# Two-layer transformer on one core: the q of layer 2's attention, and half of its k, are turned by VectorE and by transfers of lane quarters

## What is computed

```python
proj = h @ w_in[l]                          # 256 x 8704
qa, ka, va, qb, kb, vb, ga, gb = split(proj)
qa = apply_rope(rms_norm(qa, q_norm_w), cos, sin)   # 8 heads of 128
ka = apply_rope(rms_norm(ka, k_norm_w), cos, sin)   # 2 heads
ya = global_gqa(qa, ka, va)                 # 4 q heads share a k and a v head
yb = neighbourhood_attention(qb, kb, vb, rpb)       # 8 heads, a bias per head
merged = sigmoid(ga) * (ya @ w_oa) + sigmoid(gb) * (yb @ w_ob)
x = x + g1 * (merged @ w_out)               # then the feed-forward part
```

## Time and profile before

| | |
|---|---|
| Runs | 2236.20, 2235.26, 2235.86 us; median 2235.86 |
| Profiled execution | 2235.32 us, span 2233.6 us |
| TensorE busy | 2220.6 us (99%) |
| VectorE busy | 1680.4 us (75%) |
| ScalarE busy | 1104.4 us (49%) |
| Moved by DMA | 546.53 MB, mean 245 GB/s |

### The profile page before, as it was taken

The page is one execution under the profiler, slowest core; times in us unless marked ns, Lnnn a source line. Parts: engine busy times, 40 slices in busy tenths (PEclk is TensorE's granted clock), DMA queues, the critical chain, the costliest instruction groups (busy, mean ns, idle before and its releaser), DMA issues.

```text
span 2233.6 us, 31176 instructions
## 1 busy us (share of the span) xinstructions
PE 2220.6 (99%) x10287; PEld 1848.6 (83%) x10287; DVE 1680.4 (75%) x2250; ACT 1104.4 (49%) x1427; POOL 136.9 (6%) x259
## 2 busy tenths in 40 slices
PE   9999999999999999999999999999999999999998
PEld 7888888888888888888888888888888888888886
DVE  5767777878876875887788877767777777777786
ACT  6455445666664444533366653445444443444444
POOL 1100110000000000010011110000000000000000
PEclk9999999999999999999999999999999999999999
DMA  8978897666665866697689987766666676766664
GB/s 303 340 240 301 312 337 244 209 208 204 216 230 185 286 233 200 213 335 269 197 299 320 323 293 252 243 210 217 220 213 223 229 234 227 231 218 213 202 210 147
DMA packets 150219, 546.53 MB, mean 245 GB/s; under 512 B 16881, under 2 KB 17648, under 8 KB 148608
## 3 DMA queue, kind: packets, MB, share of 16 engines
q1 hardware_dynamic: 112416, 405.92, 53.7%
q0 software_dynamic: 34304, 129.64, 16.9%
q10 hardware_dynamic: 3424, 9.96, 1.1%
HBM read 534.92 MB, written 10.53 MB: 244 GB/s over the span
## 4 chain that ended last, share of the span: by engine, by line
PE 98%; DVE 1%; DMA 0%; ACT 0%; issue 0%; DVEq 0%; ACTq 0%; SPq 0%
PE ps L2072 23%; PE ps L2074 23%; PE ps L2073 23%; PE ps L2190 7%; PE ps L2192 7%; PE ps L2191 7%; PE ps L2111 2%; PE ps L2320 1%; PE ps L2087 1%; PE ps L2089 1%; PE ps L2088 1%; PE ps L2387 0%; PE ps L2388 0%; PE ps L2250 0%; PE ps L2315 0%; PE ps L2510 0%
## 5 line engine op out<-in xcount | busy, mean ns | idle before, releaser
L668 ACT ACTIVATE w_hi<-raw 128x1024 fp32r<-128x1024 f32 x749 | 790.1, 1060 | 967.7 <-PE ps L2074 820.4
L1175 DVE TENSOR_TENSOR w_lo<-raw,w_hi 128x1024 fp32r<-128x1024 f32 x757 | 922.0, 1223 | 450.5 <-ACT w_hi L668 437.3
L2072 PE MATMUL ps<-w_hi,a_hi 128*128 128x512 f32 x1612 | 629.3, 390 | 0.0
L2074 PE MATMUL ps<-w_hi,a_lo 128*128 128x512 f32 x1612 | 627.5, 389 | 0.0
L2073 PE MATMUL ps<-w_lo,a_hi 128*128 128x512 f32 x1612 | 627.3, 389 | 0.0
L2074 PEld LDWEIGHTS ps<-w_hi,a_lo 128*128 128x128 f32 x1612 | 302.5, 188 | 63.4
L2072 PEld LDWEIGHTS ps<-w_hi,a_hi 128*128 128x128 f32 x1612 | 302.6, 188 | 62.9 <-DVE a_lo L1460 0.3
L2073 PEld LDWEIGHTS ps<-w_lo,a_hi 128*128 128x128 f32 x1612 | 302.6, 188 | 61.9
L2190 PE MATMUL ps<-w_hi,a_hi 128*128 128x512 f32 x640 | 255.4, 399 | 0.0
L2192 PE MATMUL ps<-w_hi,a_lo 128*128 128x512 f32 x640 | 249.7, 390 | 0.0
L2191 PE MATMUL ps<-w_lo,a_hi 128*128 128x512 f32 x640 | 249.2, 389 | 0.0
(11 more groups left out here) (366 smaller groups left out, 2318.6 us busy)
## 6 DMA issues: line engine op xcount, KB each, us to landing
raw<-ws_dram SPq DMA_DIRECT2D x768, 512.0 KB, 4.4
ada<-wa_dram POOLq DMA_DIRECT2D x140, 512.0 KB, 4.9
late<-wa_dram POOLq DMA_DIRECT2D x35, 512.0 KB, 5.5
late_c<-wa_dram POOLq DMA_DIRECT2D x17, 512.0 KB, 5.4
gates_spill<-gst ACTq DMA_DIRECT2D x16, 512.0 KB, 5.4
ga<-gates_spill POOLq DMA_DIRECT2D x8, 512.0 KB, 4.3
gb<-gates_spill POOLq DMA_DIRECT2D x8, 512.0 KB, 5.6
bias_c<-b_merge_dram POOLq DMA_DIRECT2D x9, 256.0 KB, 5.8
```

The source lines that it names most:

```text
L668: act.activation(w_hi[:, k.slot(RING), :], raw[:, k.slot(RING), :], ACT.Copy).then_inc(hi_done, 1)
L1175: dve.tensor_tensor(w_lo[:, k.slot(RING), :], raw[:, k.slot(RING), :], w_hi[:, k.slot(RING), :].bitcast(F32), ALU.subtract).then_inc(lo_do ...
L2072: pe.matmul(o, hi(m, tb), w_hi[:, s, cols], start=m == 0, stop=False)
L2074: mm = pe.matmul(o, lo(m, tb), w_hi[:, s, cols], start=False, stop=m == of * kts - 1)
```

## The change

Five steps are changed.

1. When a chunk of q or of neighbourhood k lies in `proj`, VectorE transposes it in blocks of 32 x 32, each inside its own quarter of the lanes, into a buffer `qz` of two slots: one instruction of 128 x 512 for each half of the tokens (`q_lanes_turned`). The chunks come in the order 3, 4, 5, 0, 1, 6 (`LANES2`).
2. ScalarE waits for that (`q_lanes`) and issues 16 DMAs of 32 lanes x 1 KB, from a quarter of `qz` into a quarter of `proj[:, c]` (`quadrants`, `steps_sending`), four ahead of each of four splits. Blocks and quarters together make the 128 x 128 turn. The transfers are sent in chunks 4 to 8, one in each of chunks 4 to 7 and two in chunk 8.
3. TensorE no longer turns q in any of the four groups, nor k in the neighbourhood groups. The k of the grouped-query groups stays with it.
4. ScalarE rounds q and k from `proj` (SBUF) with a strided view, by halves of the tokens; VectorE takes the low parts from there too. Their count is the same. TensorE waits for `qk2_split` ahead of the scores.
5. Loops of ScalarE and VectorE in `proj2` are written out, and one wait of gpsimd, ScalarE's waits ahead of q_hi and of `pt_hi` (which lies on `qz`) are put to the new semaphores.

```diff
+        qz = at("qz", SC + 8 * K, [P, 2, 4, TB, 4, 32])
+        def heads_first(c):
+            return proj[:, c].rearrange("p t n -> p (t n)").rearrange("p (i t h s) -> p t h i s", i=4, t=TB, h=4)
+        def lanes(x, tb):
+            return x[:, :, tb * P:(tb + 1) * P].rearrange("p h (i s) -> p h i s", i=4)
...
-        gqa = Attention("gqa", 2, 1, 2 + 4)
-        na = Attention("na", 2, 1, 2 + 2 + 4)
+        gqa = Attention("gqa", 2, 1, 4)
+        na = Attention("na", 2, 1, 4)
+        SPLIT2 = {"gqa": (0, 2), "na": (2 * gqa.groups, 4)}
+        LANES2 = (3, 4, 5, 0, 1, 6)
+        TURN_DMAS = 4 * 4 * 16
...
                     if m == 3 * N_LATE + 1:
-                        pool.wait_ge(t_done, TG["na"] + 4)
+                        pool.wait_ge(qk2_split, SPLIT2["na"][0] + 4)
...
# ScalarE, attention
+                else:
+                    if a.kind == "gqa" and g.base == 0:
+                        act.wait_ge(q_turned[0], 2 * TURN_DMAS)
+                        act.wait_ge(q_turned[1], 3 * TURN_DMAS)
+                    elif g.base == 0:
+                        act.wait_ge(gqa.qk_done, len(gqa.units) * gqa.groups)
+                    else:
+                        act.wait_ge(a.qk_done, nu)
+                    for tb in range(TB):
+                        act.activation(lanes(q_hi, tb), heads_first((3 if na_ else 0) + i)[:, tb], ACT.Copy).then_inc(qk2_hi, 1)
...
                 if na_:
-                    for h in range(2):
-                        act.wait_ge(t_done, (r + 1).n)
-                        act.activation(k2_hi[:, 2 * h:2 * h + 2, :], ps[:, 4 + r.slot(2), :], ACT.Copy)\
-                            .then_inc(qk2_hi, 1)
-                        r = r + 1
+                    act.wait_ge(q_turned[0], 3 * TURN_DMAS)
+                    for tb in range(TB):
+                        act.activation(lanes(k2_hi, tb), heads_first(5 + i)[:, tb], ACT.Copy).then_inc(qk2_hi, 1)
...
                     elif j and not nsa_:
+                        act.wait_ge(q_turned[0], 3 * TURN_DMAS)
...
# ScalarE, projection
-            with act.Fori(1, 6) as i:
+            def quadrants(n):
+                act.wait_ge(q_lanes, n + 1)
+                s = (n + 1) % 2
+                turned = proj[:, LANES2[n]].rearrange("p t n -> p (t n)").rearrange("p (i r) -> p i r", i=4)
+                z = qz[:, s].rearrange("p b t h s -> p b (t h s)")
+                def column(b):
+                    for i in range(4):
+                        act.dma_start(turned[32 * b:32 * b + 32, i, :], z[32 * i:32 * i + 32, b, :]).then_inc(q_turned[s], 16)
+                return column
+            def steps_sending(k, n):
+                column = quadrants(n)
+                for b in range(4):
+                    column(b)
+                    steps(k + b, 1)
+            with act.Fori(1, 4) as i:
                 steps(At(T0["proj2"], T_K, i), T_K)
+            k = At(T0["proj2"] + 4 * T_K)
+            steps(k, 3)
+            steps_sending(k + 3, 0)
+            steps(k + 7, 1)
+            k = k + T_K
+            steps(k, 1)
+            steps_sending(k + 1, 1)
+            steps(k + 5, 3)
...
+            k = k + T_K
+            steps_sending(k, 4)
+            steps_sending(k + 4, 5)
...
# VectorE, projection
+            def q_lanes_turned(n):
+                c, s = LANES2[n], (n + 1) % 2
+                if n >= 2:
+                    dve.wait_ge(q_turned[s], n // 2 * TURN_DMAS)
+                for tb in range(TB):
+                    ins = dve.transpose(qz[:, s, :, tb], proj[:, c, tb].rearrange("p (h b f) -> p b h f", h=4, b=4))
+                ins.then_inc(q_lanes, 1)
...
             for c in range(3):
                 k, g = k + T_K, g + 1
+                dve.wait_ge(acc_free, G0["proj2"] + 5 + c + 3)
+                q_lanes_turned(2 + c)
                 steps(At(k), 2)
                 qk_scaled(c)
                 steps(At(k + 2), 2)
                 qk_turned(c, 0)
+                if c == 2:
+                    q_lanes_turned(5)
                 steps(At(k + 4), 2)
                 qk_turned(c, 1)
                 steps(At(k + 6), 2)
...
# TensorE, attention
-                for h in range(2):
-                    turn(r, [q[:, tb, 2 * h + m, :] for m in range(2) for tb in range(TB)]).then_inc(t_done, 1)
-                    r = r + 1
+                if nsa_:
+                    for h in range(2):
+                        turn(r, [qr[:, tb, 2 * h + m, :] for m in range(2) for tb in range(TB)]).then_inc(t_done, 1)
+                        r = r + 1
...
-                if na_:
-                    k_ = proj[:, 5 + i].rearrange("p t (h d) -> p t h d", h=4)
-                    for h in range(2):
-                        turn(r, [k_[:, tb, 2 * h + m, :] for m in range(2) for tb in range(TB)]).then_inc(t_done, 1)
-                        r = r + 1
...
                 else:
+                    pe.wait_ge(qk2_split, SPLIT2[a.kind][0] + SPLIT2[a.kind][1] * (g.base + 1))
                     pe.wait_ge(proj_in, 1)
```

More of the change, by code:

```diff
@@ L349, in build @@
         qk2_hi, v2_hi_done, v2_split, pt_hi_done = sem("qk2_hi"), sem("v2_hi_done"), sem("v2_split"), sem("pt_hi_done")
+        q_lanes, q_turned, qk2_split = sem("q_lanes"), [sem(f"q_turned{k}") for k in range(2)], sem("qk2_split")
         hdn_ready, hdnT_done, hdnT_ready, w2_in = sem("hdn_ready"), sem("hdnT_done"), sem("hdnT_ready"), sem("w2_in")
@@ L1318, in k_rest @@
                 def k_rest():
-                    for h in range(2):
-                        hs = slice(2 * h, 2 * h + 2)
-                        rest(k2_lo[a.kind][:, hs, :], 2 + h, 4 + (TG[a.kind] + g.base * a.tg + h) % 2, k2_hi[:, hs, :], t_free)
+                    for tb in range(TB):
+                        rest(lanes(k2_lo[a.kind], tb), 2 + tb, heads_first(5 + i)[:, tb], lanes(k2_hi, tb), qk2_split)
                 def p_rest(j):
@@ L1326, in p_rest @@
                         dve.wait_ge(pt_hi_done, u + 1)
-                        dve.tensor_tensor(pt_lo[:, n, :], ps[:, 4 + (TG["gqa"] + g.base * a.tg + 2 + 2 * (j - 1) + n) % 2, :],
+                        dve.tensor_tensor(pt_lo[:, n, :], ps[:, 4 + (TG["gqa"] + g.base * a.tg + 2 * (j - 1) + n) % 2, :],
                                           pt_hi[:, n, :].bitcast(F32), ALU.subtract).then_inc(t_free, 1)
@@ L1783, in _ @@
             n = ADA_TURN["proj2"][0]
-            with dve.Fori(0, 2) as i:
-                for c in range(2):
-                    k = At(T0["proj2"] + (c + 1) * T_K, 2 * T_K, i)
-                    steps(k, T_K, At(ADA0["proj2"] + c * n // 2, n, i), n // 2, c * n // 2)
-                    copy_out(2 * i + (c + 1), k, At(G0["proj2"] + (c + 1), 2, i))
-                keep_modulation(At(ADA0["proj2"], n, i), n, At(KEPT0["proj2"], 1, i))
+            def q_lanes_turned(n):
+                c, s = LANES2[n], (n + 1) % 2
+                if n >= 2:
+                    dve.wait_ge(q_turned[s], n // 2 * TURN_DMAS)
+                for tb in range(TB):
+                    ins = dve.transpose(qz[:, s, :, tb], proj[:, c, tb].rearrange("p (h b f) -> p b h f", h=4, b=4))
+                ins.then_inc(q_lanes, 1)
+            for i in range(2):
+                for c in range(2):
+                    k = At(T0["proj2"] + (2 * i + c + 1) * T_K)
+                    a, na_ = At(ADA0["proj2"] + i * n + c * n // 2), n // 2
+                    if (i, c) == (1, 1):
+                        steps(k, 2, a, 2, c * n // 2)
+                        dve.wait_ge(acc_free, G0["proj2"] + 3 + 3)
+                        q_lanes_turned(0)
+                        steps(k + 2, T_K - 2, a + 2, na_ - 2, c * n // 2 + 2)
+                    else:
+                        steps(k, T_K, a, na_, c * n // 2)
+                    copy_out(2 * i + (c + 1), k, At(G0["proj2"] + (2 * i + c + 1)))
+                keep_modulation(At(ADA0["proj2"] + i * n), n, At(KEPT0["proj2"] + i))
             dve.wait_ge(trig2_in, 32)
@@ L2200, in attention @@
                 fill(a.fill[0] - between)
-                q = qr if nsa_ else proj[:, (3 if na_ else 0) + i].rearrange("p t (h d) -> p t h d", h=4)
                 if not na_:
                     pe.wait_ge(a.q_ready, (g + 1).n)
-                for h in range(2):
-                    turn(r, [q[:, tb, 2 * h + m, :] for m in range(2) for tb in range(TB)]).then_inc(t_done, 1)
-                    r = r + 1
+                if nsa_:
+                    for h in range(2):
+                        turn(r, [qr[:, tb, 2 * h + m, :] for m in range(2) for tb in range(TB)]).then_inc(t_done, 1)
+                        r = r + 1
                 if not na_:
```

31 lines of the change are left out of this document (17 added, 14 removed).

## The result

The changed kernel takes 2240.86 us in the median of eleven executions (2238.1 to 2243.9) against 2235.86 for the kernel before, a ratio of 1.0020 with a 95% interval of 1.0012 to 1.0029. It is slower by 0.2%, where the prediction said 2230.8 us (range 2229.9 to 2234.8) and had 0.50 on faster. The profiled execution took 2238.95 us, its span 2237.1.

A forecast was written before the change was run, and what follows sets the result against it. TensorE, busy for 99% of the span, was taken to bound the kernel. From the median 2235.86 us, 5.5 saved, 0.3 added for the k-turn wait and 0.1 for the scores gave 2230.8 us, range 2229.9 to 2234.8.

The forecast's parts named there:

- What is added: Part pricing the new work: VectorE's twelve transposes at 0.70 us, ScalarE's 96 DMA issues at 0.36 us, and resulting waits.
- the bound of 0.50: ScalarE's DMA issue: upper bound of 0.50 us each, from the 256-row issue and a gap.
- the far bound of 0.68: ScalarE's DMA issue: extreme of 0.68 us each, from the gpsimd row and a gap.
- the lane quarters: VectorE's transposes: quarters one after another, about 2.3 us each, losing about 13.5 us; 0.10 together with slow issues.
- the walk through chunk 8: New order laid on old starts, tile by tile: first gate tile's split 0.9 us ahead of need, k turns wait 0.3.
- slower by the issues: Rival: issues at 0.68 us lose 12 us in chunks 5 to 8 and first group, 2242.8; 0.10 with slow quarters.
- The saving: TensorE without 48 of the 52 turns reading `proj`: 5.5 us saved (5.3 to 5.7), all on the path.
- the two kept turns: Two turns of grouped-query k staying on TensorE in each of its two groups, taken at 0.30 us.
- the low parts: VectorE's low parts of q and k in the attention: as many as before, at 0.68 us.
- the landing: Last gqa q transfer issued by 1102.7, wanted at 1117.4; rival that transfers land late, 2253 us, had 0.04.
- the increment that runs ahead of the copy: `gqa_q_ready` before the k turns: VectorE's sequencer runs ahead, so it comes at 1115.7 to 1116.6, TensorE waiting 0 to 0.6.
- I cost it at nothing, and 0.5 us at worst: Weight loads in the shorter neighbourhood groups: DMA engines always wanted, but tiles still over 2 us ahead of TensorE.

The follow-up runs named there:

- e_order: Changed kernel with one rounding put ahead of each wait for the transposed lanes in chunk 8, all issues still on ScalarE: 2235.72 us, ratio 0.9995.
- e_fill: Changed kernel plus 16 extra matmuls on TensorE, result unused, ahead of the first gate tile: 2242.93 us, ratio 1.0029.
- e_last: Changed kernel with only chunk 8's two transfers (32 issues) moved from ScalarE to GpSimd: 2231.91 us, ratio 0.9978.
- e_pool: Changed kernel with all 96 transfers issued by GpSimd instead of ScalarE: 2231.96 us, ratio 0.9978.
- e_order_fill: `e_order` plus eleven extra matmuls, result unused, behind the first gate tile where TensorE stood for 2.5 us: 2234.67 us, ratio 0.9999.
- e_second: `e_last` with the second transfer of chunk 8 (16 issues) back on ScalarE: 2236.61 us, ratio 1.0005.

## Why the prediction was wrong

**The step that failed** is in "What is added": "with a gap between two I take 0.36 us, so 1.44 us for four". It is 0.612 us and 2.44 to 2.46 us. I had scaled a single issue to DRAM by the number of its rows, and the rows don't count. The true value lies between the bound of 0.50 and the far bound of 0.68, to which I gave a tenth with the lane quarters. Everything in the walk through chunk 8 follows from that term: with 0.612 us in it the same walk has the second transfer at 1112.2 and the split of the first gate tile at 1115.7 (an estimate), near the measured 1112.52 and 1116.15. ScalarE still keeps pace in steady state (2.56 us from rounding to rounding against 2.72), since it does issue while it works. But the first wait puts it 2.44 us behind instead of 1.4, and the second transfer starts at 1112.52 instead of 1108.8. The split of the first gate tile starts at 1116.15, where 1111.4 was forecast and 1113.46 is when its result is needed. `gqa.q_ready` comes at 1123.9 instead of 1115.7 to 1116.6. The rival "slower by the issues" had the mechanism and, at 0.68 us, 2242.8 (its 12 us lost add up to 2242.4).

**The term that was missing** is the granted clock behind a gap. It made the second loss in chunk 8's timeline, which the wait for the k turn covers in the first profile of the changed kernel (nothing in the sum). In the second profile it adds 1.3 us, in `e_order` 1.2, in `e_fill` 2.5.

**One distance orders the versions without the turns.** It is the one from the time at which the first gate matmul is due (the last projection matmul and 0.227 us, or its start where it is on time) to the first score matmul, in the profiled execution. The third column is the median of `e_last` and the difference of the distances.

| version | distance, us | 2231.91 and the difference | median measured |
|---|---|---|---|
| `e_last` | 8.44 | | 2231.91 |
| `e_pool` | 8.43 | 2231.9 | 2231.96 |
| `e_order_fill` | 11.57 | 2235.0 | 2234.67 |
| `e_order` | 12.76 | 2236.2 | 2235.72 |
| `e_second` | 13.48 | 2236.9 | 2236.61 |
| changed kernel, two executions | 16.55, 17.87 | 2240.0, 2241.3 | 2240.86 |
| `e_fill` | 19.27 | 2242.7 | 2242.93 |

The medians come out within 1 us. But the distance is that of one execution, the medians are of several sets, and single executions differ by more in other places: from its own profiled times (2230.97 for `e_last`) the same sum gives 2236.0 for `e_second`, measured 2233.65, and 2234.1 for `e_order_fill`, measured 2231.97. So the table shows that the loss is in this stretch, and not its size to some tenths.

Of the changed kernel's 16.55 - 8.44 = 8.1 us, 4.05 are the first gap, 2.4 the slow tile, 1.3 the wait for the k turn and 0.3 what follows. With `e_fill` and `e_pool` together it is shown that the first three are one delay, ScalarE's, under which a shorter gap only makes a longer wait.

**What held.** The saving: in the changed kernel itself the second grouped-query group takes 8.44 us from gate to scores (1172.83 to 1181.27), and the neighbourhood groups 10.88 and 10.98 (1224.07 to 1234.95, 1275.95 to 1286.93), where the earlier trace rows has 9.30, 12.70 and 12.90. The first group in `e_pool` takes 8.43. That is 0.87 + 0.86 + 1.82 + 1.92 = 5.5 us, the forecast value, and the two kept turns are 8.44 - 8.16 = 0.28 (forecast 0.30). The transposes at 0.692 us (0.70), the low parts at 0.685, the landing (ScalarE rounds q at 1124.66 right behind its last weight rounding, with no wait for a DMA), and the increment that runs ahead of the copy. The landing has its harder test in `e_pool`, where ScalarE rounds q at 1117.32, where the forecast had it, and doesn't wait either.

**What was costed too low:** "I cost it at nothing, and 0.5 us at worst", of the loads in the first neighbourhood group. Over the two neighbourhood groups it was 2.2 and 1.6 us in the two executions looked at closely, and something in seven of ten. That can hold the 1.2 us by which `e_pool` (2231.96) stays above the forecast of 2230.8. What decides whether an execution has this wait stays open, and so does what the first 2.0 us of the slower execution hang on: its trace has TensorE standing 1.6 us for a `w_lo` in the stretch from 180 to 236 us, where the faster one doesn't stand.

## What to carry to other kernels

The cost of a DMA for the engine that issues it is time in its queue, which its busy share doesn't show: ask what stands behind the issue before choosing the engine, and price it from a row with the same two ends (SBUF or DRAM) issued in the same sequence, not by its size. Here an idle queue made the same transfers free, and the change worth 3.8 us instead of costing 5.0. A gap in TensorE had two prices here, its length and the matmuls at half clock behind it; and where two waits of one cause follow one another, filling the first only moved the loss to the second.

## What the runs showed of the hardware that I had not expected

- On ScalarE an issue within SBUF takes 0.61 us in a run of four and 0.47 alone, one to DRAM 0.44 to 0.51 and 0.34; within SBUF rows (32 or 128) and bytes (256 to 1,024 a row) change it by 0.01 us. The 0.47 is from transfers of 128 rows alone. The same transfer issued by GpSimd takes 0.496 us.
- ScalarE's issues run beside its arithmetic: the rounding at 1099.78 and the next issues at 1099.80 overlap for 1.04 us.
- Behind gaps of 2.2 to 4.3 us six to twelve matmuls stood 0.427 us apart, and the changed kernel had twelve of them in one execution and seven in another behind the same gap of 4.05 us.
